# Two sample states of each head placed in the buffer of the prompt's values

## The reference

```python
proj = jnp.einsum('bld,dp->blp', h, w_in)
...
    b = jnp.cumsum(ac, axis=1)
    ...
    scores = jnp.sum(qc[:, :, None] * kc[:, None, :] * decay, axis=-1)
    o_intra = jnp.einsum('btsh,bshv->bthv', scores, vc)
    o_inter = jnp.einsum('bthk,bhkv->bthv', qc * jnp.exp(b), S)
    k_dec = kc * jnp.exp(b_last[:, None] - b)
    S_new = jnp.exp(b_last)[..., None] * S + jnp.einsum('bshk,bshv->bhkv', k_dec, vc)
...
o = rmsnorm(o, gla_norm_g)
```

## Time and profile before

| | |
|---|---|
| median of 3 runs | 2538.51 us |
| lowest and highest | 2530.4 and 2538.56 us |
| profiled execution, its own time | 2533.12 us |
| its span in the trace | 2531.4 us |
| PE busy | 2484.1 us (98%) |
| DVE, ACT, POOL busy | 1789.1 (71%), 1066.9 (42%), 216.1 us (9%) |
| DMA traffic | 350.30 MB, mean 138 GB/s |

### The profile page before, as it was taken

How to read it: one execution, slowest core, us unless ns; L and a number is a source line. 1 busy time by engine, 2 the same in 40 slices (tenths; PEclk the granted TensorE clock), 3 DMA queues, 4 the chain that set the end, 5 groups by cost and what they waited for, 6 DMA issues and landing times.

```text
span 2531.4 us, 44463 instructions
## 1 busy us (share of the span) xinstructions
PE 2484.1 (98%) x18552; PEld 2444.7 (97%) x18552; DVE 1789.1 (71%) x2537; ACT 1066.9 (42%) x1558; POOL 216.1 (9%) x369
## 2 busy tenths in 40 slices
PE   8999999999999999999999999999999999999996
PEld 7999999999999999999999999999999999999996
DVE  5448657586588878788787888876668778885223
ACT  5344444443444434443443444444445445334222
POOL 2002012020120000000000011100000101111000
PEclk8999999999999999999999999999999999999998
DMA  6225325153354433334443346654569768557332
GB/s 197 71 64 161 110 86 180 53 167 111 110 163 113 117 101 103 106 92 118 117 114 94 101 129 177 177 143 124 167 194 287 226 203 284 148 163 223 83 83 75
DMA packets 443805, 350.30 MB, mean 138 GB/s; under 512 B 13828, under 2 KB 416688, under 8 KB 439632
## 3 DMA queue, kind: packets, MB, share of 16 engines
q1 hardware_dynamic: 412560, 231.69, 33.2%
q0 software_dynamic: 31056, 115.91, 13.7%
HBM read 277.65 MB, written 69.91 MB: 137 GB/s over the span
## 4 chain that ended last, share of the span: by engine, by line
PE 90%; DVE 4%; DMA 3%; issue 1%; ACT 1%; SPq 0%; POOL 0%; ACTq 0%; DVEq 0%
PE bank L1548 32%; PE acc L1548 25%; PE acc L1466 18%; PE acc L419 6%; PE acc L1370 2%; PE acc L1434 1%; PE bank L1398 1%; DMA raw<-in_w_out 1%; PE bank L1431 1%; DMA raw<-in_w_in 1%; DVE ring_lo L1699 1%; PE bank L1428 1%; PE acc L1565 1%; PE bank L1402 0%; DVE act_x L2257 0%
## 5 line engine op out<-in xcount | busy, mean ns | idle before, releaser
L1699 DVE TENSOR_TENSOR ring_lo<-pa,ring_hi 128x1024 fp32r<-128x1024 f32 x476 | 581.8, 1222 | 186.4 <-ACT ring_hi L903 183.6
L903 ACT ACTIVATE ring_hi<-pa 128x1024 fp32r<-128x1024 f32 x476 | 502.6, 1056 | 362.9 <-PE bank L1548 207.4
L1466 PE MATMUL acc<-act_y,w_hi 128*128 128x288 f32 x2560 | 519.6, 298 | 0.0
L1548 PE MATMUL bank<-act_x,ring_hi 128*128 128x288 f32 x2240 | 439.0, 294 | 0.8 <-ACT act_x L1188 0.6
L1548 PE MATMUL bank<-act_y,ring_hi 128*128 128x288 f32 x2112 | 415.0, 295 | 0.0
L1466 PEld LDWEIGHTS acc<-act_y,w_hi 128*128 128x128 f32 x2560 | 412.1, 189 | 2.9 <-issue 1.2
L1548 PE MATMUL acc<-act_x,ring_hi 128*128 128x288 f32 x1984 | 396.4, 294 | 1.3 <-DVE ring_lo L1699 1.3
L1466 PE MATMUL acc<-act_y,w_lo 128*128 128x288 f32 x1280 | 378.6, 296 | 0.0
L1548 PEld LDWEIGHTS bank<-act_x,ring_hi 128*128 128x128 f32 x2240 | 357.4, 189 | 1.3 <-ACT act_x L1188 0.8
L1548 PEld LDWEIGHTS bank<-act_y,ring_hi 128*128 128x128 f32 x2112 | 335.7, 189 | 0.5 <-DVE act_y L2301 0.3
L1548 PEld LDWEIGHTS acc<-act_x,ring_hi 128*128 128x128 f32 x1984 | 320.0, 189 | 1.5 <-issue 1.5
(11 more groups left out here) (322 smaller groups left out, 3186.4 us busy)
## 6 DMA issues: line engine op xcount, KB each, us to landing
pa<-in_w_in SPq DMA_DIRECT2D x208, 512.0 KB, 5.2
raw<-in_w_in SPq DMA_DIRECT2D x40, 1024.0 KB, 5.7
states<-in_state_gla POOLq DMA_DIRECT2D x64, 256.0 KB, 3.1
out<-states POOLq DMA_DIRECT2D x64, 256.0 KB, 2.9
pa<-in_w_branch_a SPq DMA_DIRECT2D x32, 512.0 KB, 6.0
pa<-in_w_branch_b SPq DMA_DIRECT2D x32, 512.0 KB, 5.1
raw<-in_w_out SPq DMA_DIRECT2D x16, 1024.0 KB, 5.9
gate_tile<-gate_d POOLq DMA_DIRECT2D x32, 288.0 KB, 3.5
```

The source lines that it names most:

```text
L903: A(ring_hi[g % RING][:, :], piece_of[src][u % 2][:, :], ACT.Copy).then_inc(part_hi, 1)
L1466: mm = nc.tensor.matmul(half_bank[h % 2][:, 0:HALF], (w_hi, w_lo)[a][par][:, k * P:(k + 1) * P], y_of(k, b, j), start=(k == 0 and n == 0), ...
L1548: mm = nc.tensor.matmul(out, (ring_hi, ring_lo)[a][r][:, k * P:(k + 1) * P], slot_of(slot, b)[:, k, :], start=(p in (0, 1, 3) and k == 0 a ...
L1699: V.tensor_tensor(ring_lo[g % RING][:, :], piece_of[SOURCE[p]][u % 2][:, :], ring_hi[g % RING][:, :].bitcast(F32), ALU.subtract).then_inc( ...
```

## The change

`STATE_AT` gives each sample of a head a place. Samples 0, 2 and 6 share place 0, samples 1, 3 and 7 share place 1, as parts of `states`. Samples 4 and 5 have places 2 and 3, and these are `v_rows` 0 and 1, and 2 and 3: the memory of the prompt's values. Nothing is added to the memory in use.

```diff
+        STATE_AT = (0, 1, 0, 1, 2, 3, 0, 1)
+        def state_of(j):
+            n = STATE_AT[j]
+            return states[:, n, :, :] if n < 2 else v_rows[:, (n - 2) * KK:(n - 1) * KK, :]
+        def states_before(i, j):
+            return i * STATE_AT.count(STATE_AT[j]) + STATE_AT[:j].count(STATE_AT[j])
...
             def load_state(i, j):
                 rows = state_gla[0, j, i, :, :].rearrange("(k p) v -> k p v", p=P)
+                n, before = STATE_AT[j], states_before(i, j)
+                if n >= 2:
+                    pool.wait_ge(chunk_mm, i * NCH + NT)
                 for kk in range(KK):
-                    if NS * i + j >= 2:
-                        pool.wait_ge(st_out[j % 2][kk], 8 * NS * i + 16 * (j // 2))
-                    pool.dma_start(states[:, j % 2, kk, :], rows[kk]).then_inc(st_in[j % 2], 16)
+                    if before:
+                        pool.wait_ge(st_out[n][kk], 16 * before)
+                    pool.dma_start(state_of(j)[:, kk, :], rows[kk]).then_inc(st_in[n], 16)
...
+                i = head_at(h, AT_CHUNK[NT - 1] + 1)
+                if i is not None:
+                    load_state(i, 4)
+                    load_state(i, 5)
                 i, j = bit_at(h - 2, AT_SEQ)
                 if i is not None:
                     rows = new_gla_sample[0, j, i, :, :].rearrange("(k p) v -> k p v", p=P)
                     for kk in range(KK):
                         pool.wait_ge(seq_upd, (i * NS + j) * KK + kk + 1)
-                        pool.dma_start(rows[kk], states[:, j % 2, kk, :]).then_inc(st_out[j % 2][kk], 16)
-                    if j + 2 < NS:
-                        load_state(i, j + 2)
+                        pool.dma_start(rows[kk], state_of(j)[:, kk, :]).then_inc(st_out[STATE_AT[j]][kk], 16)
+                    if j in (0, 1, 2, 3):
+                        load_state(i, (2, 3, 6, 7)[j])
...
                 two = bank[:, 0:2, :].rearrange("p b c -> p (b c)")
+                if i and m == 0:
+                    for n in (2, 3):
+                        for kk in range(KK):
+                            act.wait_ge(st_out[n][kk], 16 * i)
                 A(v_rows[:, :, m * P:(m + 1) * P], two[:, 0:NCH * P].rearrange("p (t c) -> p t c", c=P), ACT.Copy
```

More of the change, by code:

```diff
@@ L303, in hybrid_kernel @@
         key_hi, kd_hi, seq_kd, seq_mm, seq_upd = sem("key_hi"), sem("kd_hi"), sem("seq_kd"), sem("seq_mm"), sem("seq_upd")
-        st_in = [sem(f"st_in{n}") for n in range(2)]
-        st_out = [[sem(f"st_out{n}{k}") for k in range(2)] for n in range(2)]
+        st_in = [sem(f"st_in{n}") for n in range(4)]
+        st_out = [[sem(f"st_out{n}{k}") for k in range(2)] for n in range(4)]
         inter_saved, chunk_mm, chunk_sq, chunk_state, sp_out = (
@@ L678, in _ @@
             pool.dma_start(gate_d[0, GATE_UNITS - 1], mix_tile[:, 1, :]).then_inc(extra_out, 16)
-            for n in range(2):
+            for n in range(4):
                 for kk in range(KK):
-                    pool.wait_ge(st_out[n][kk], 16 * (NS // 2) * H)
+                    pool.wait_ge(st_out[n][kk], 16 * STATE_AT.count(n) * H)
             pool.wait_ge(sp_out, 16 * H)
@@ L989, in seq_round @@
             def seq_round(i, j):
-                act.wait_ge(st_in[j % 2], KK * (i * (8 * NS) + 16 * (j // 2 + 1)))
+                act.wait_ge(st_in[STATE_AT[j]], 16 * KK * (states_before(i, j) + 1))
                 if j:
@@ L996, in seq_round @@
                     act.wait_ge(chunk_mm, i * NCH)
-                A(s_hi[:, :, :], states[:, j % 2, :, :], ACT.Copy).then_inc(state_hi, 1)
+                A(s_hi[:, :, :], state_of(j), ACT.Copy).then_inc(state_hi, 1)
                 act.wait_ge(seq_kd, i + 1)
@@ L1813, in sample_update @@
                 for kk in range(KK):
-                    st = states[:, j % 2, kk, :]
+                    st = state_of(j)[:, kk, :]
                     V.scalar_tensor_tensor(out=st, in0=st, scalar=decay_end[:, kk, NT + j:NT + j + 1],
@@ L1830, in sample_split @@
                 dve.wait_ge(state_hi, i * NS + j + 1)
-                V.tensor_tensor(s_lo[:, :, :], states[:, j % 2, :, :], s_hi[:, :, :].bitcast(F32),
+                V.tensor_tensor(s_lo[:, :, :], state_of(j), s_hi[:, :, :].bitcast(F32),
                                 ALU.subtract).then_inc(seq_split, 1)
@@ L1999, in _ @@
                 if h == NH - 4:
-                    for r in range(2):
+                    for r in range(4):
                         for kk in range(KK):
-                            dve.wait_ge(st_out[r][kk], 16 * (NS // 2) * H)
+                            dve.wait_ge(st_out[r][kk], 16 * STATE_AT.count(r) * H)
                     dve.wait_ge(o_ready, NCH * H)
```

## The result

The changed kernel takes 2578.36 us (median of 4 runs, 2576.15 to 2580.12) against 2537.66 (4 runs, 2530.4 to 2538.56): the medians are 40.7 us apart. The ratio, estimated from the single runs and not the quotient of the two medians, is 1.0175, with a 95% interval of 1.0157 to 1.0192; that would be 44 us. It is slower, as forecast. The profiled execution took 2580.12 us, 47.0 more than the one of before.

The account below looks back on a forecast made before the run. PE, busy 98% of the span, was taken to bound the kernel. Four heads at 9.1 + 1.5 us, less 1.5, gave 40.9 us on the profiled 2533.1, or 2574; forecast 2575, range 2559 to 2592.

Parts of the forecast that it names:

- No slack, nothing to win: At sample 3, any delay of DVE's remainder delays PE equally; the change can directly give back only 1.5 us.
- The 1.5 us at sample 7: PE's wait for sample 7's operands in the last head, 1.5 us, forecast to be given back.
- The cause: POOL's queue order: waiting for chunk 3 and four loads now precede sample 1's store, sample 3's load and chunk 1's output.
- Steps 1 and 2: After chunk 3 ends on PE, POOL sees the semaphore (0.3 us) and issues four loads (2.3 us).
- Step 3: Sample 1's store must land before sample 3's load: 8.1 us after chunk 3's end, bounds 6.8 to 9.5.
- Steps 4 and 5: Chunk 1's output lands 12.3 us after chunk 3's end; ACT copies and rounds, DVE's remainder starts at 13.9.
- A head's stall: DVE's remainder moves from 4.8 to 13.9 us after chunk 3: 9.1 us lost per head, bounds 7.7 to 10.6.
- The clock: PE's clock drops behind each stall, costing 1.5 us per head, bounds 0 to 1.9; 6 us in all.
- Sum: Four heads' stall and clock losses less 1.5 us given back: 40.9 us on the profiled execution's 2533.1, giving 2574.
- The store beside the weights: 256 KB of POOL's queue took 1.4 us longer beside SP's weights; landing takes 3.8 instead of 2.4 us.
- What I put at nothing: ACT's new wait before the next head's first `v_rows` copy, and POOL's backlog, caught up by number 23: no cost.

Follow-up runs that it names:

- the second trace of the changed kernel: The changed kernel run again unaltered, beside later runs of the kernel before: 2579.72 us, ratio 1.0175.
- the wait alone: Kernel before plus only POOL's wait for chunk 3 ahead of sample 1's store, no state in the values' tile: 2565.17 us, ratio 1.0121.
- only the output behind: Changed kernel with sample 1's store and sample 3's load moved ahead of the wait and four loads, chunk 1's output still behind: 2562.37 us, ratio 1.0111.
- transposes: Changed kernel plus 60 unused transposes of 128 columns on PE ahead of sample 3, in the stall: 2583.65 us, ratio 1.0192 to the kernel before.
- the matmuls: Changed kernel plus 60 unused matmuls of 288 columns on PE ahead of sample 3, in the stall: 2576.31 us, ratio 1.0167 to the kernel before.
- the loads last: Changed kernel with loads for samples 4 and 5 moved behind sample 1's store, sample 3's load and chunk 1's output: 2532.53 us, ratio 0.9991 to kernel before.

## Why the prediction was right

The forecast was 2575 us in a range of 2559 to 2592, and the time is 2578.

- **No slack, nothing to win.** Right. Every us by which DVE's remainder came later was passed to PE's mean (10.6 and 10.6). The 1.5 us at sample 7 came back; with the order mended they are all there is.
- **The cause.** Right, and shown from both sides: with the same wait, places and bytes, the order alone restores the time; and the wait without the loads, put ahead of the store, loses some 70% of it (ratios 1.0121 and 1.0175).
- **Steps 1 and 2** (POOL sees C, four loads): 2.7 us forecast, 2.4 measured.
- **Step 3** was mis-sized: sample 3's load at C + 8.1 forecast, C + 9.3 to 9.5 measured, the upper bound. And its reasoning was off. I had taken the disturbed time from store to load as one that counts from the issue, whenever that is. The runs show that a store issued at C + 0.3 beside the weights takes 5.6 us, against 3.8 for the one issued 2.2 us later in the kernel before: nothing of it moves in the first 2 us of the weights' traffic. Without the weights the queue's own loads alone hold sample 3's load back to C + 7.8. The costs that I had as a base and an addition overlap.
- **Steps 4 and 5.** The output landed 3.4 us after its issue; I had 3.0, the 2.7 of an output and a little. With the 1.2 us of step 3 the remainder came at C + 15.4, not 13.9. That the output, more than the load, would be what is waited for was right; the load, issued by 398.7 and landed 2.9 us later by the trace, lands about a us before it.
- **A head's stall**: 9.1 forecast (7.7 to 10.6), 10.6 to 10.9 measured: at the upper bound or just over it in every head.
- **The clock**: 6.0 us forecast, 6.1 measured; but spread otherwise, 0, 2.0, 1.6 and 2.5 instead of 1.5 each. The 1.5 was the 3.62 less 2.16 us of the earlier trace rows, where the slower 16 matmuls stood behind an idle time of 2.11 us and the clock had been granted at 0.50; the upper bound of 1.9 was my estimate. In the first head the slow stretch ended with the stall (0.50 up to 242 us, 1.00 from 244, the mean at 243.70). That the sum fits so well is luck: the second trace of the changed kernel has 2.5, 1.9, 1.6 and 2.3, 8.3 in all. Nor does the cost follow the length of PE's stall: waits of 5.8 to 6.0 us cost 0, 1.6, 0 and 0 in the wait alone, waits of 4.1 to 4.3 us cost 1.9 to 2.3 in each head with only the output behind.
- **Sum**: 40.9 forecast on the profiled execution, 47.0 measured, the rest in steps 3 and 4, times four. The median lies nearer, within 3 us, partly by luck: the sum was 6 us too small, but the profiled execution of before lay 4.5 us under its median and that of the changed kernel 1.8 over its own, so that the medians are 40.7 apart. Added to the median instead of the profiled execution, the same sum would have given 2579.
- **The store beside the weights.** The prediction has 1.4 us more for it there, 3.8 us to landing instead of 2.4. In the wait alone, where it is issued 0.3 us behind the weights, it took 5.6 us, without them 2.5. The weights themselves took 7.1 us to land, 5.7 in the kernel before. Why nothing of the store moves before C + 3, no run shows.
- **What I put at nothing** (ACT's wait at the next head's first copy, POOL's backlog): right. After number 22 PE has no wait in the heads' stretch that it had not before, and ACT waits no longer for its first `v_rows` copies than before (9.0 us in all against 9.2).

## What to carry to other kernels

A load that is moved forward is free only if nothing that somebody waits for stands behind it in its queue. Before adding a wait to an engine that issues DMAs, list what it issues after that wait and when each is needed: here the same two loads, put last in the same step, cost nothing instead of some 40 to 45 us. And a store whose landing gates the next load should be priced by what else is in flight at that moment, its own queue's loads and the other queues' alike: here it landed in 2.5 us alone, in 5.6 beside the weights, in 5.2 behind the loads. Those prices overlapped (6.6 us with both, where the sum gives 8.3), so measure them together.

## What the runs showed of the hardware

- A sample's store from POOL (two transfers of 256 KB) lands in 2.4 to 2.5 us alone, 5.6 beside 1 MB of weights issued 0.3 us before it, 5.2 behind 1 MB of loads in its own queue, 6.6 with both.
- Halving the loads ahead of the store (1 MB to 512 KB) left the wait for its landing unchanged beside the weights, 5.88 against 5.79 us; it was issued 1.1 us earlier, and landed about 1 us earlier.
- The granted clock stayed at 1.00 through 6.7 us of nothing but transposes, and fell to 0.5 behind a gap of 2.63 us; after the matmuls, behind two gaps of 1.36 and 2.33 us, it fell in one head of four, though the gaps in the others were as long (1.4 to 1.7 and 2.3).
- The granted clock also fell to 0.5 with PE busy throughout: once in the trace of the kernel before (432.6 to 439.4 us, at a cost of 3.2 us), once in that of the changed kernel (786 to 789.5 us), twice in that with the loads last (277 to 285 and 591 to 599 us). Each time it fell within 0.6 us of the end of the last chunk's 16 small matmuls (half 26; 64 columns each, 2.8 us together), in some heads and not in others; why in those, stays open. The spread of the kernel before goes with the clock: its runs with a mean of 0.994 took 2528 to 2532 us, those with 0.990 2537 to 2542.
